# Two neighbouring VectorE steps change places in the attention tiles behind the short convolution

## What is computed

```python
def short_gated_conv(zb, conv_w, norm_g):
    bg, cg, hv = jnp.split(zb, 3, axis=-1)
    y = bg * depthwise_conv(cg * hv, conv_w)
    return rms_norm(y, norm_g)

def block(qb):                       # inside diff_attention, 128 queries
    s = jnp.einsum("bqhcd,bkhcd->bhcqk", qb, k).astype(jnp.float32)
    p = jax.nn.softmax(s, axis=-1)
    w = p[:, :, 0] - lam * p[:, :, 1]
    return jnp.einsum("bhqk,bkhe->bqhe", w, v.astype(jnp.float32))

        mix = jnp.concatenate([ya, yb, yc], axis=-1) @ w_out[l]
        x = x + g1[:, None, :] * mix
        h = modulate(rms_norm(x, norm2_g[l]), sh2, sc2)
        x = x + g2[:, None, :] * swiglu(h, w_gate_up[l], w_down[l])
```

## Time and profile before

| | us |
|---|---|
| median of 3 runs (1191.63 to 1191.93) | 1191.85 |
| the profiled execution, its own time | 1192.22 |
| its span in the trace | 1190.40 |
| TensorE busy | 1177.7 (99%) |
| VectorE busy | 715.0 (60%) |
| ScalarE busy | 502.8 (42%) |
| GpSimd busy | 118.5 (10%) |

### The profile page before, as it was taken

One profiled execution on the slowest core, in us unless ns is written; L12 is line 12 of the kernel. 1 busy time (PEld: TensorE's weight loads), 2 busy tenths in 40 slices (PEclk: granted clock), 3 DMA queues, 4 the chain that ended last, 5 costly groups with the idle time before them and its releaser, 6 DMA issues.

```text
span 1190.4 us, 14437 instructions
## 1 busy us (share of the span) xinstructions
PE 1177.7 (99%) x5186; PEld 932.1 (78%) x5186; DVE 715.0 (60%) x1036; ACT 502.8 (42%) x763; POOL 118.5 (10%) x195
## 2 busy tenths in 40 slices
PE   9999999999999999999999999999999999999998
PEld 6787556878888888888888876677888888888887
DVE  7989998985555433466667988757733333332221
ACT  5546788453232323222243458866523232332220
POOL 2321232120102000211000112100000000000000
PEclk9999999999999999999999999999999999999999
DMA  8788346886665222777413764423332322323322
GB/s 304 245 240 182 74 104 194 302 271 207 194 194 174 91 99 95 283 247 247 141 55 123 162 139 92 86 54 106 106 99 95 98 96 91 103 90 107 105 104 88
DMA packets 48940, 175.18 MB, mean 147 GB/s; under 512 B 5697, under 2 KB 5825, under 8 KB 48898
## 3 DMA queue, kind: packets, MB, share of 16 engines
q1 hardware_dynamic: 30386, 107.13, 27.2%
q0 software_dynamic: 18512, 67.51, 20.4%
HBM read 172.52 MB, written 2.10 MB: 147 GB/s over the span
## 4 chain that ended last, share of the span: by engine, by line
PE 90%; DVE 5%; ACT 3%; issue 1%; POOL 0%; ACTq 0%; DVEq 0%; POOLq 0%
PE ps L1617 22%; PE ps L1619 22%; PE ps L1618 22%; PE ps L1677 4%; PE ps L1679 4%; PE ps L1678 4%; PE ps L1646 3%; PE ps L1650 2%; PE ps L1866 1%; ACT prob L755 1%; DVE neg_max L1264 1%; PE ps L1662 1%; PE ps L1663 1%; PE ps L1667 1%; PE ps L1841 1%
## 5 line engine op out<-in xcount | busy, mean ns | idle before, releaser
L629 ACT ACTIVATE w_hi<-raw 128x1024 fp32r<-128x1024 f32 x196 | 207.5, 1060 | 537.3 <-PE ps L1619 467.5
L1010 DVE TENSOR_TENSOR w_lo<-raw,w_hi 128x1024 fp32r<-128x1024 f32 x164 | 201.3, 1228 | 252.6 <-ACT w_hi L629 250.3
L1617 PE MATMUL ps<-h_hi,w_hi 128*128 128x512 f32 x832 | 329.0, 395 | 0.0
L1619 PE MATMUL ps<-h_lo,w_hi 128*128 128x512 f32 x832 | 324.1, 390 | 0.0
L1618 PE MATMUL ps<-h_hi,w_lo 128*128 128x512 f32 x832 | 324.0, 389 | 0.0
L1617 PEld LDWEIGHTS ps<-h_hi,w_hi 128*128 128x128 f32 x832 | 156.2, 188 | 48.3 <-issue 17.4
L1619 PEld LDWEIGHTS ps<-h_lo,w_hi 128*128 128x128 f32 x832 | 156.2, 188 | 32.7
L1618 PEld LDWEIGHTS ps<-h_hi,w_lo 128*128 128x128 f32 x832 | 156.3, 188 | 31.6 <-issue 0.5
L1617 PE MATMUL ps<-gu_hi,w_hi 128*128 128x512 f32 x352 | 136.9, 389 | 0.0
L1618 PE MATMUL ps<-gu_hi,w_lo 128*128 128x512 f32 x352 | 136.9, 389 | 0.0
L1619 PE MATMUL ps<-gu_lo,w_hi 128*128 128x512 f32 x352 | 136.9, 389 | 0.0
(11 more groups left out here) (214 smaller groups left out, 1393.4 us busy)
## 6 DMA issues: line engine op xcount, KB each, us to landing
raw<-w_stream SPq DMA_DIRECT2D x196, 512.0 KB, 3.3
w_lo<-w_stream POOLq DMA_DIRECT2D x32, 512.0 KB, 8.0
ada_ring_gu<-ada POOLq DMA_DIRECT2D x28, 512.0 KB, 4.4
ada_ring_late<-ada POOLq DMA_DIRECT2D x28, 512.0 KB, 4.8
ada_ring_first<-ada POOLq DMA_DIRECT2D x16, 512.0 KB, 5.1
ada_ring_mid_a<-ada POOLq DMA_DIRECT2D x12, 512.0 KB, 5.1
ada_ring_mid_b<-ada POOLq DMA_DIRECT2D x12, 512.0 KB, 5.1
xT<-x_t SPq DMA_DIRECT2D x4, 512.0 KB, 5.6
```

What stands on the lines that cost most here:

```text
L629: act.activation(w_hi[:, u % RING, :], raw[:, u % RAW, :], ACT.Copy).then_inc(s_whi, 1)
L1010: dve.tensor_tensor(w_lo[:, u % RING, :], raw[:, u % RAW, :], w_hi[:, u % RING, :].bitcast(F32), ALU.subtract).then_inc(s_wlo, 1)
L1617: pe.matmul(dst, whi, rhs[0][:, n, :], start=start, stop=False)
L1619: return pe.matmul(dst, whi, rhs[1][:, n, :], start=False, stop=stop)
```

## The change

In the tiles whose number is one above an entry of `CONV_AT`, which are tiles 5 and 11 of each layer, VectorE issues `row_mix_in(it)` ahead of `row_max(it+1)`; in the other 14 tiles the order stays. Nothing is added or removed, and the queues of the other engines are untouched.

```diff
--- before.py
+++ after.py
@@ -1432,9 +1432,13 @@
                 conv_a_taps(l, TAPS_FIRST[l])
                 row_inverse(l, 0)
                 for it in range(N_TILES):
+                    behind_conv = it - 1 in CONV_AT
+                    if behind_conv:
+                        row_mix_in(l, it)
                     if it + 1 < N_TILES:
                         row_max(l, it + 1)
-                    row_mix_in(l, it)
+                    if not behind_conv:
+                        row_mix_in(l, it)
                     taps = TAPS_TILE[l][it]
                     conv_a_taps(l, min(taps, 1))
                     if it + 1 < N_TILES:
```

## The result

The changed kernel takes 1194.72 us (median of 12 runs, 1194.28 to 1195.61), the kernel before, run beside it, 1191.65 us (median of 12 runs). The ratio is 1.0024, with a 95% interval from 1.0017 to 1.0032: 3.07 us slower, where 1.2 had been forecast.

The account below looks back on a forecast made before the run. TensorE, busy 99% of the span, was taken as the bound. Stalls removed (-1.59 us) less time given back at tiles 7, 12 and 14 made +1.17, some +1.2: 1193.0 us against the median, range 1190.9 to 1194.8.

Parts of the forecast that it names:

- What bounds the kernel: Whole span: TensorE is busy 99%, other engines 60% or less, so only time when TensorE stands still can be won.
- Tile 5: Both layers: the mixing step starts without a wait and TensorE's stall goes, worth 0.91 and 0.68 us, 1.59 together.
- Given back at tile 7: Transposes of tile 7 wait because the maximum comes 0.67 later: 1.08 us lost, leads of 0.23 and 0.28 left.
- Tile 11: Mixing step, bound by ScalarE, starts no earlier, gain zero; tile 12's exponentials come 1.88 us later in layer 0.
- Tile 12: TensorE's transposes wait for the late mixing step: 0.56 us given back in layer 0, 0.76 in layer 1.
- The rest of the attention: Layer 0 after tile 12: ScalarE's 1.13 us idle at tile 13 cuts the delay of 1.88 to about 0.75.
- The term for tile 14: Layer 0: transposes of tile 14 allowed at 186.44, wanted at 186.08, so another 0.36 us is lost.
- The sum: Whole kernel: -1.59, +1.08, +0.56, +0.76 and +0.36 give +1.17 us, some +1.2; chance 0.68.
- rival (2): Tiles 13 and 14: the 1.88 us delay of each layer reaches TensorE whole, +3.8 us, 1195.6; chance 0.14.
- The first: Rival: tile 11 costs nothing, its delay hidden in slack; 0.5 us gained (1191.3), at best 1.6 (1190.3); chance 0.18.
- The third: Rival: tile 5's early step is blocked by the short convolution or GpSimd's factor; only costs, 1193.6; within the forecast's 0.68.
- The rule on the queues: Trainium skill: "ACT/DVE are strict FIFO", so at tile 11 the row maximum must wait behind the mixing step.

Follow-up runs that it names:

- e9: Kernel before with the exchange at tile 5 only and one long-convolution tap moved from tile 5 to tile 4, both layers: 1190.16 us against 1191.84.
- e1: Kernel before with the exchange at tile 5 of each layer alone, tile 11 as before: 1191.36 us against 1191.91.
- e10: Kernel before with one long-convolution tap moved from tile 5 to tile 4 in both layers, no exchange: 1192.24 us against 1191.79.
- e3: Whole change, with ScalarE's copy of head 1's output put ahead of tile 13's exponentials: 1192.95 us against 1191.91 for the kernel before.
- e2: Kernel before with the exchange at tile 11 of each layer alone, tile 5 as before: 1194.77 us against 1191.91.
- e8: Kernel before with the mixing step ahead of the row maximum in all 16 tiles of each layer: 1231.36 us against 1191.84.

## Why the prediction was right or wrong

**What bounds the kernel.** Right. TensorE's busy time is the same within 1.4 us, and the 2.6 us that the attention adds are waits of TensorE and what follows them.

**Tile 5.** Right to 0.01 in layer 0. The stall is gone in both layers: 0.59 us across the three rows where a bare passage takes 0.58, so 0.90 won; in layer 1 it is 0.59 as well (731.43 to 732.02), 0.67 won. e9, which keeps all of it, ends at 0.90 and 0.64.

**Given back at tile 7.** Right: the lead that is left is 153.53 + 0.22 - 153.52 = 0.23 in layer 0, to the hundredth, and in layer 1 it is 1.61 - (741.40 - 740.06) = 0.27 for 0.28. Part of it was given back a tile earlier than I had said (the 0.18 at 148.91), which the sum doesn't notice. e1 ends with -0.23 and -0.25, and e9 and e10 show that it is the one round of VectorE that takes it back.

**Tile 11.** Right. The mixing step starts no earlier: 169.67 less the 0.22 of the start is 169.45, the number of the text. It waits 1.05 us in layer 0 and 1.70 in layer 1 instead of 0.55 and 0.57, and the exponentials are 171.65 - 169.55 - 0.22 = 1.88 late.

**Tile 12.** Right: the first row of transposes that waits stands at 177.05 - 176.55 - 0.22 = 0.28 behind where 0.27 was worked out (0.33 with the 0.06 behind it), and in layer 1 764.32 - 762.25 - 1.61 = 0.46 for 0.42. One wait there the sum put at nothing: TensorE's scores of tile 14 start at 760.54 against 759.00, when the exponentials of tile 12 are done, and are 0.19 later by it. It costs nothing further, because the transposes behind them wait in any case.

**"The rest of the attention."** This is the step that failed. It says that ScalarE's 1.13 us of idle time at tile 13 takes the chain's delay down to about 0.75, and goes from there to tile 14. That cover is on ScalarE behind the copy of head 1's output, and TensorE waits for the copy. I followed only the ring (maximum, exponentials, reciprocal, scaling, mixing) through the in-order queues, and left out what else stands in them. All rows for it were in the trace of before: the copy ends at 175.66 + 0.59 = 176.25, with 1.88 at 178.13; the product starts 0.15 us behind the copy's end (178.51 - 178.36 in after), so at 178.28 instead of 176.99, 1.29 us late. Measured: 1.30. Layer 1: 761.21 + 0.62 + 1.88 + 0.15 = 763.86 against 762.68, 1.18 late; measured 1.16. In place of +0.69 and +0.48 the sum would have been about +1.3 and +1.2, which is +2.5 or 1194.3.

**The term for tile 14.** Its +0.36 is right only where the copy doesn't come first. In after tile 14 adds nothing: TensorE is 179.54 - 177.94 = 1.60 behind right after the product that waited for the copy, and 187.36 - 185.75 = 1.61 at tile 14's transposes, both with the start's 0.22. In e3, where the copy is out of the way, it goes from 0.33 to 0.68.

**The sum.** +1.17 by the working, some 2.6 by the traces, 2.78 and 3.07 by the two pairs of medians. 1.4 us of the miss are the copy by the traces (e3 against the change: 0.71 and 0.7), 1.7 to 2.0 by the medians. What lies between the traces' 2.6 and the medians I can't assign. The start of the kernel, ahead of attention, varies by up to half a microsecond between traces, and I haven't found what makes it vary. The measured 1194.72 lies inside the stated range by 0.08 us only. That upper end came from half the price of rival (2) and not from the mechanism that made the time, so the range held by luck. Of the signs named beforehand the waits at tiles 5, 7 and 12 and the idle time at tile 11 came; the statistic and the last projection are late by 1.39 instead of the 0.5 to 0.7 that the list gave.

**The rivals.** The first (tile 11 costs nothing) is ruled out by e2. The second put its price at tile 13, which was the right place, but for the wrong reason: it had the delay reach the transposes of tiles 13 and 14 whole through the statistic. Its condition came true in part. ScalarE's idle time ahead of that `L802` is 0.63 in after, 1.13 before, so only 0.50 of the cover was used, because the statistic was late with TensorE:

```profile
184.02 0.69 ACT L802 ACTIVATE rstd<-ps,eps 128x512 f32<-128x512 f32 x1 [0.63 <-PE ps L1727]
```

But TensorE was late there because the copy had stopped it ahead of that, and nothing was added behind: the transposes of tiles 13 and 14 are 1.61 late, the same as the product before them. The third, that the early step at tile 5 does not start early, is ruled out by its row: 142.13 - 0.22 = 141.91, as worked out. The result, +3.07 us or 0.24%, falls into the class "slower by over 0.2%", which had a chance of 0.15, all of it from the second rival and the forecast's upper side; the mechanism that came true had no chance of its own in my list. **The rule on the queues** held everywhere: in no trace did the maximum pass the mixing step, and the decisive wait is an instruction, the copy, that needed nothing from the late ones and stood behind them.

## What to carry to other kernels

An instruction may be put ahead of another in an in-order queue where all that it reads is there already, as at tile 5; where it would wait, as at tile 11, the other now waits with it, for nothing. Even at tile 5 the other was later by 0.67 us, which took back 1.08 of the 1.59 us won until that time was freed elsewhere (e9). To price such a delay, write down everything that stands in each delayed queue for the next round or two, also what has nothing to do with the chain, and ask of each whether the engine that sets the end waits for it. The same reading shows the better version: idle time ahead of an instruction that waits for another engine is where a movable one goes (e9), and a copy that nobody holds up belongs ahead of the one that may be late (e3).

## What the runs showed of the hardware that was not expected

**A short stall of TensorE costs more than the idle time that the profile shows.** At tile 5 the trace shows 0.68 idle, and 0.90 us came back when it went. Most of the difference lies in how rows overlap: a matmul row ahead of the transposes lasts 0.40 and the next starts 0.23 after it, so the idle time is counted from 0.17 later than the point at which the next could have started. The other 0.06 is the later start of the row behind the one that waited. Behind the wait of 0.81 for the copy the two products took 1.10 where they take 1.02, and started 0.15 us after the copy's end.

**In e8 the granted clock fell behind TensorE's waits.** Stretches of layer 0 with the wait of 2.02 and the one of 2.60 and what followed them; the columns are the length, the busy time of PE, PEld, DVE, ACT and POOL with their counts, the granted clock, the share of DMA and GB/s:

```profile
131.90:133.90 2.00, 0.05 (x1) 0.00 (x0) 1.13 (x2) 1.43 (x5) 0.00 (x0) 0.83 0.00 0
133.97:136.05 2.08, 2.08 (x5) 0.58 (x5) 1.52 (x4) 1.99 (x3) 1.84 (x2) 0.50 0.18 24
137.00:142.00 5.00, 5.00 (x19) 3.48 (x17) 4.09 (x7) 3.49 (x7) 1.25 (x1) 0.70 0.73 152
160.00:165.00 5.00, 5.00 (x21) 2.57 (x19) 3.52 (x6) 3.49 (x7) 2.09 (x2) 1.00 0.29 96
...
167.65:169.70 2.05, 2.05 (x4) 0.55 (x4) 1.28 (x3) 1.61 (x3) 0.93 (x1) 0.50 0.39 76
```

TensorE stood still in the first stretch, ran at 0.50 of full speed (1.2 GHz) in the second, and was not back at 1.00 in the third. Its timeline over the second wait shows the price:

```profile
167.65 2.05 PE L1870 MATMUL ps<-w_t,v 128*128 128x512 f32 x2 [2.60 <-ACT oc L782]
```

Two products took 2.05 us instead of 1.02. In after the mean granted clock of the run is 1.0; its longest wait of TensorE is followed by matmuls at full speed. These are the wait and, in columns as above, what came behind it:

```profile
830.74 1.12 PE L1707 MATMUL ps<-sq_sum,ones 128*128 128x512 f32 x2 [1.35 <-DVE sq_sum L1319]
...
830.70:832.70 2.00, 1.96 (x9) 1.41 (x10) 0.64 (x1) 0.77 (x2) 0.00 (x0) 1.00 0.00 0
```

So a stall in a kernel that is bound by TensorE can cost its own length, as in the changed kernel, or well over it, as in e8.
